# One chain per tile on compact 64x64 blocks, a modulation ring of its own, and the last expert added from PSUM

## The reference, cut to what matters

```python
cs = jax.nn.silu(c)
for l in range(DEPTH):
    mod = (cs @ w_ada[l] + b_ada[l])[:, None, :]
    sh1, sc1, gt1, sh2, sc2, gt2 = jnp.split(mod, 6, axis=-1)
    h = rmsnorm(x, norm_mix[l]) * (1 + sc1) + sh1
    x = x + gt1 * mixer(h, ...)
    h = rmsnorm(x, norm_ffn[l]) * (1 + sc2) + sh2
    x = x + gt2 * (swiglu(h, ...) if l % 2 == 0 else moe(h, ...))
y = rmsnorm(x, norm_final) * (1 + scf) + shf
...
# gated delta-net, chunks of 64 tokens
m = jnp.where(strict, beta_h[..., :, None] * kk * lmask, 0.0)
t_inv = lax.linalg.triangular_solve(eye + m, eye, left_side=True, lower=True, unit_diagonal=True)
u = jnp.einsum('bnhts,bnshv->bnthv', t_inv, v * beta[..., None])
...
# experts
for e in range(N_EXPERTS):
    y = y + combine[..., e:e + 1] * swiglu(h, w_gate[e], w_up[e], w_down[e])
```

## Time and profile before

| | us |
|---|---|
| median of 3 executions | 2027.31 (2026.44 to 2028.02) |
| profiled execution, its own time | 2026.02 |
| its span in the trace | 2024.2 |
| TensorE busy (share of the span) | 1890.4 (93%) |
| VectorE busy | 1449.0 (72%) |
| ScalarE busy | 1100.7 (54%) |
| GpSimd busy | 12.6 (1%) |

### The profile page before, as it was taken

The page is one execution under the profiler, slowest core; times in us unless marked ns, Lnnn a source line. Parts: engine busy times, 40 slices in busy tenths (PEclk is TensorE's granted clock), DMA queues, the critical chain, the costliest instruction groups (busy, mean ns, idle before and its releaser), DMA issues.

```text
span 2024.2 us, 25108 instructions
## 1 busy us (share of the span) xinstructions
PE 1890.4 (93%) x10235; PEld 1552.2 (77%) x10235; DVE 1449.0 (72%) x1760; ACT 1100.7 (54%) x1101; POOL 12.6 (1%) x27
## 2 busy tenths in 40 slices
PE   5997899899999978987999999999999999999995
PEld 2995667899989956665778787787877878878783
DVE  2857647645448667476888788787887888888884
ACT  3754223333337642324667676775766767666772
POOL 0000000000000000000000000000000000000000
PEclk7997899999999988997999999999999999999997
DMA  9445374343352443732989899898998989989980
GB/s 374 155 138 180 123 265 156 136 147 115 128 197 105 149 177 107 276 135 103 365 331 349 326 355 335 330 355 319 354 341 326 361 325 339 351 318 362 334 316 27
DMA packets 92119, 505.29 MB, mean 250 GB/s; under 512 B 8064, under 2 KB 8224, under 8 KB 40544
## 3 DMA queue, kind: packets, MB, share of 16 engines
q1 hardware_dynamic: 89616, 488.29, 65.4%
q0 software_dynamic: 2384, 15.34, 2.0%
HBM read 494.88 MB, written 8.72 MB: 249 GB/s over the span
## 4 chain that ended last, share of the span: by engine, by line
issue 55%; PE 31%; DVE 10%; ACT 2%; SPq 1%; DMA 1%; POOL 0%; DVEq 0%; ACTq 0%; POOLq 0%
PE bank L610 30%; DVE wlo L424 1%; DVE work L1715 1%; DMA raw<-in_w_in 1%; SPq L524 1%; DVE wscr L1867 1%; PE bank L834 1%; ACT work L1248 0%; DVE work L1716 0%; DVE wscr L1939 0%; ACT L1248 0%; ACT whi L419 0%; SPq L533 0%; DVE work L1847 0%; DVE hl L1646 0%
## 5 line engine op out<-in xcount | busy, mean ns | idle before, releaser
L424 DVE TENSOR_TENSOR wlo<-raw,whi 128x2048 fp32r<-128x2048 f32 (+1 forms) x412 | 919.9, 2262 | 198.9 <-ACT whi L419 197.3
L419 ACT ACTIVATE whi<-raw 128x2048 fp32r<-128x2048 f32 (+1 forms) x412 | 761.7, 1889 | 79.8 <-PE bank L610 75.4
L610 PE MATMUL bank<-whi,hg_high 128*128 128x512 f32 x896 | 368.7, 411 | 1.5 <-DVE hg_low L2129 1.5
L610 PE MATMUL bank<-whi,hg_low 128*128 128x512 f32 x896 | 354.8, 396 | 0.0
L610 PE MATMUL bank<-wlo,hg_high 128*128 128x512 f32 x896 | 354.5, 396 | 0.0
L610 PE MATMUL bank<-hh,whi 128*128 128x320 f32 x944 | 298.5, 316 | 23.4 <-DVE hl L1637 17.2
L610 PE MATMUL bank<-hh,wlo 128*128 128x320 f32 x944 | 293.6, 311 | 0.0
L610 PE MATMUL bank<-hl,whi 128*128 128x320 f32 x944 | 293.5, 311 | 0.0
L1248 ACT ACTIVATE work<-bank 128x512 f32<-128x512 f32 (+3 forms) x217 | 101.0, 487 | 262.3 <-PE bank L610 231.8
L610 PEld LDWEIGHTS bank<-hh,whi 128*128 128x128 f32 x944 | 179.6, 190 | 30.9 <-issue 22.3
L610 PEld LDWEIGHTS bank<-whi,hg_high 128*128 128x128 f32 x896 | 168.8, 188 | 43.1 <-issue 4.4
(11 more groups left out here) (262 smaller groups left out, 1860.6 us busy)
## 6 DMA issues: line engine op xcount, KB each, us to landing
raw<-in_moe SPq DMA_DIRECT2D x336, 1024.0 KB, 4.8
raw<-in_ada SPq DMA_DIRECT2D x56, 1024.0 KB, 5.4
raw<-in_w_in SPq DMA_DIRECT2D x30, 1024.0 KB, 4.8
raw<-in_gu SPq DMA_DIRECT2D x22, 1024.0 KB, 4.8
raw<-in_down SPq DMA_DIRECT2D x16, 704.0 KB, 4.0
raw<-in_w_out SPq DMA_DIRECT2D x8, 1024.0 KB, 5.2
work<-in_s_gdn POOLq DMA_DIRECT2D x2, 2048.0 KB, 12.2
out_gdn_s<-work POOLq DMA_DIRECT2D x2, 2048.0 KB, 7.4
```

The costliest lines, as they stand in the source:

```text
L419: ac.activation(whi[:, part(n), 0:width(n)], raw[:, n % SLOTS, 0:width(n)], ACT.Copy).then_inc(S("w_high"), 1)
L424: ve.tensor_tensor(wlo[:, n % SLOTS, 0:width(n)], raw[:, n % SLOTS, 0:width(n)], whi[:, part(n), 0:width(n)], ALU.subtract).then_inc(S("w_ ...
L610: return pe.matmul(out, lhsT, rhs, start=start, stop=stop, **k)
```

## The change

**Inversion.** Tiles 0 and 1 now have one chain each. Up to v = 5 it works on the two diagonal 64x64 blocks of each head alone: the block of rows 0 to 63 and that of rows 64 to 127 stand in the same 256 columns, four heads side by side. TensorE handles the blocks one by one, alternating between the quarter of the array with rows and columns 0 to 63 and that with rows and columns 64 to 127; the transposes of the second quarter are products with the identity. One mask and one update on DVE, and one copy on ACT, cover all four heads. Level 6 (`LAST`) only computes the 64x64 block that lies off the diagonal: four transposes, four products, ACT's copy, four products, and a negation on DVE. Some set-up is added (a unit block, a copy of the level table, a cleared quarter), and the strict matrix is written in blocks.

**Modulation.** Each modulation group and weight has its place in a list, `RING`, from which SP issues. Group 1 stays ahead of the inversion of layer 0 and group 2 in its levels. Group 3 has six loads behind the sums of squares of layer 0's output, two in the dense FFN (u = 2 and 3), and its turn at u = 5. Group 4 has six behind the sums of squares of the dense FFN, two in layer 1's projection (u = 3 and 4), its turn at u = 8. Group 5 stands ahead of layer 1's inversion. Group 6 has six behind the sums of squares of layer 1's output and two at the start of the experts.

**End.** The residual of experts 0 to 6 runs on DVE in the last expert, the last expert goes from PSUM into x, the flag is loaded before that, the squares and their sums come ahead of the branch, and y is stored in four parts.

```diff
+def ring_order():
+
+    def ada(x, *ks):
+        yield from (("ada", x, k) for k in ks)
+
+    def weights(first, n):
+        yield from (("w", first + i) for i in range(n))
+
+    yield from ada(0, *range(KD))
+    yield from weights(AT_IN[0], H_IN)
+    yield from ada(1, *range(KD))
+    yield from ada(2, *range(KD))
+    yield from weights(AT_OUT[0], H_OUT)
+    for x, first, n in ((3, AT_GU, H_GU + H_DN), (4, AT_IN[1], H_IN)):
+        yield from ada(x, 0)
+        yield from weights(first, 1)
+        yield from ada(x, 1, 2, 3, 4, 5)
+        yield from weights(first + 1, 3)
+        yield from ada(x, 6, 7)
+        yield from weights(first + 4, n - 4)
+    yield from ada(5, *range(KD))
+    yield from weights(AT_OUT[1], H_OUT)
+    yield from ada(6, *range(KD))
+    yield from weights(AT_MOE, len(MOE))
...
-        IBANK = (NB[0:2], NB[2:4], XB[1:2])
+        IBANK = (NB[0], NB[1], XB[1])
+        INV = [(t[4][:, 256:], t[4][:, 0:256], t[5][:, 0:256], t[5][:, 256:], t[7]) for t in DSET[0:2]]
+        INV.append((DSET[2][3], DSET[2][4], DT2[:, 0:256], DU2[:, 0:256], DY2))
...
-        ABANK = B[1]
+        ABANK = [B[1], B[1], B[1], B[7], B[3], B[1], B[7]]
...
-            yield from ((i, hs, v) for i in range(2) for hs in range(2))
+            yield from ((i, v) for i in range(2))
             if 2 <= v < 2 + LEVELS[2]:
-                yield 2, 0, v - 2
-
-        def chain(i, hs):
-
-            nt = TILES[i][1]
-            heads = (2 * hs, 2 * hs + 1) if i < 2 else range(NH)
-            return nt, heads, slice(heads[0] * nt, (heads[-1] + 1) * nt), IBANK[i][hs]
+                yield 2, v - 2
...
+            for at, what in enumerate(RING):
+                if at >= SLOTS:
+                    gone = RING[at - SLOTS]
+                    if gone[0] == "w":
+                        sp.wait_ge(*used(gone[1]))
+                    else:
+                        sp.wait_ge(S("ada_mm"), KD * gone[1] + gone[2] + 1)
...
-            po.wait_ge(S("y_done"), 1)
-            store(O["y"], hT[:], "y_out")
+            po.wait_ge(S("hs_norm"), 5)
+            for k in range(1, KD, 2):
+                po.wait_ge(S("h_norm"), KD + k + 1)
+                store(O["y"][:, k - 1:k + 1, :], hT[:, k - 1:k + 1, :], "y_out")
...
+                    def turned(o, m, r):
+
+                        return mm(o, m, ident[r, r]) if r.start else pe.transpose(o, m, ident[r, r])
...
+                            bank, (_, MB, TC, UC, YC) = IBANK[i], INV[i]
+                            if (i, x) in AT_MASK:
...
+                            if x == LAST:
+                                DM, DU = DSET[i][3], DSET[i][6]
+                                for h in range(NH):
+                                    pe.transpose(bank[0:64, 64 * h:64 * h + 64], DU[0:64, P * h:P * h + 64], ident[0:64, 0:64])
+                                for h in range(NH):
+                                    ins = mm(bank[0:64, 256 + 64 * h:320 + 64 * h], DM[64:P, P * h:P * h + 64],
+                                             DU[64:P, P * h + 64:P * h + P])
+                                ins.then_inc(S("dy_mm"), 1)
+                                continue
+                            for h in range(NH) if x > 1 else ():
+                                for r in blocks(i):
+                                    turned(bank[r, 64 * h:64 * h + 64], UC[r, 64 * h:64 * h + 64], r)
+                            for h in range(NH):
+                                for r in blocks(i):
+                                    o, m = bank[r, 256 + 64 * h:320 + 64 * h], MB[r, 64 * h:64 * h + 64]
+                                    if x:
+                                        ins = mm(o, m, UC[r, 64 * h:64 * h + 64])
+                                    else:
+                                        ins = turned(o, m, r)
                             ins.then_inc(S("dy_mm"), 1)
-                        for i, hs, x in chains(v):
+                        for i, x in chains(v):
                             if x == 0:
                                 continue
-                            nt, heads, _, bank = chain(i, hs)
-                            DT, DY = DSET[i][5], DSET[i][7]
-                            after(pe, "dy", l, AT_UPDATE[i, hs, x])
-                            for h in heads:
-                                c = slice(h * nt, (h + 1) * nt)
-                                o = (h - heads[0]) * nt
-                                ins = mm(bank[0:nt, o:o + nt], DT[0:nt, c], DY[0:nt, c])
+                            bank, (_, MB, TC, UC, YC) = IBANK[i], INV[i]
+                            after(pe, "dy", l, AT_UPDATE[i, x])
+                            for h in range(NH):
+                                for r in blocks(i) if x < LAST else (slice(0, 64),):
+                                    c = slice(64 * h, 64 * h + 64)
+                                    ins = mm(bank[r, c], TC[r, c], YC[r, c])
...
-                        ada(x + 1, *((0,), (1, 2), (3, 4), (5, 6), (7,))[v - 2])
+                    if v > 1 and l == 0:
+                        ada(2, *((0,), (1, 2), (3, 4), (5, 6), (7,))[v - 2])
...
-                ada_turn(x + 1)
+                if l == 0:
+                    ada_turn(2)
                 heads_spread(("heads", 2 * l + 1))
                 after(pe, "gdn_state", l, 1)
                 new_values(1)
-                ada(x + 2, 0)
                 keys(2)
-                ada(x + 2, 1)
                 after(pe, "do", l, 1)
                 outputs(1)
-                ada(x + 2, 2, 3)
                 new_values(2)
-                ada(x + 2, 4)
                 after(pe, "do", l, 2)
                 outputs(2)
-                ada(x + 2, 5)
                 after(pe, "do", l, 3)
                 heads_sum(("heads", 2 * l + 2), w(4 * TL, TL))
-                ada(x + 2, 6, 7)
                 heads_spread(("heads", 2 * l + 2))
-                ada_turn(x + 2)
...
+                ada((3, 6)[l], 0, 1, 2, 3, 4, 5)
                 if l == 0:
 
                     for u in range(FD):
@@ -1018,6 +1055,10 @@
                                 ins = mm3(B[2 * b + u % 2][:, 0:T], wh[:, k, c], wl[:, k, c], hh[:, k, :], hl[:, k, :],
                                           k == 0, k == KD - 1)
                         ins.then_inc(S("gu_mm"), 1)
+                        if u in (2, 3):
+                            ada(3, u + 4)
+                        if u == 5:
...
+                    ada(4, 0, 1, 2, 3, 4, 5)
...
+            for j in range(KD):
+                sum_squares(5, hT, j)
...
-                def masked(i, hs, v):
-
-                    (nt, heads, c, _), (DM, DMB) = chain(i, hs), DSET[i][3:5]
-                    nh = len(heads)
+                def masked(i, v):
+
+                    nt, (MC, MB, _, _, _) = TILES[i][1], INV[i]
                     if v:
-                        after(ve, "dy_mm", l, AT_LEVEL[i, hs, v - 1])
-                    lev = v3(cbf("level", nt), 7)
-                    do(tt(v3(DMB[0:nt, c], nh), v3(DM[0:nt, c], nh), mid(lev[:, v, 0:nt], nh), ALU.mult), "dmb")
+                        after(ve, "dy_mm", l, AT_LEVEL[i, v - 1])
+                    lev = v3(cbf("level", nt), 7)[:, v, 0:64]
+                    do(tt(v3(MB[0:nt, 0:256], 4), v3(MC[0:nt, 0:256], 4), mid(lev, 4), ALU.mult), "dmb")
...
+                            if x == LAST:
+                                do(ts(full[0:64, :, 64:], v3(bank[0:64, 0:256], 4), -1.0, None, ALU.mult), "dtu")
+                            elif i < 2 and x == LAST - 1:
+                                for r in blocks(i):
+                                    ins = tt(full[r, :, r], v3(UC[r, :], 4), v3(bank[r, 0:256], 4), ALU.subtract)
+                                    go(ins) if r.start == 0 else do(ins, "dtu")
+                            else:
+                                do(tt(UC[0:nt, :], UC[0:nt, :], bank[0:nt, 0:256], ALU.subtract), "dtu")
...
+                if e == NE - 1 and c in (3, 4) and (kind, b) in SPREAD:
+                    j = 4 * (c - 3) + SPREAD.index((kind, b))
+                    ve.wait_ge(S("e_scatter"), KD * (NE - 1))
+                    residual(hT[:, j, :], j, 48 + 40, None)
...
+            more = ve.value_load(flag[0:1, 0:1], min_val=0, max_val=1)
             for j in range(KD):
-                ve.wait_ge(S("e_sc_mm"), KD * (NE - 1) + j + 1)
-                scattered(j, B[4 + j % 2]).then_inc(S("e_scatter"), 1)
-            ve.wait_ge(S("e_scatter"), KD * NE)
-
-            more = ve.value_load(flag[0:1, 0:1], min_val=0, max_val=1)
+                n, bank, gate = KD * (NE - 1) + j + 1, B[4 + j % 2], md(48 + 40)
+                xs = v3(xT[:, j, TP:], NSEQ)
+                ve.wait_ge(S("e_sc_mm"), n)
+                go(stt(xT[:, j, 0:TP], bank[:, 0:TP], gate[:, j, 0:1], xT[:, j, 0:TP], ALU.mult, ALU.add))
```

(3 more changed lines are left out.)

293 lines of the change are left out of this document (154 added, 139 removed).

## The result

The changed kernel takes 2042.26 us (median of four, 2037.9 to 2048.93); the kernel before, in the same runs, 2027.06. The ratio is 1.0078 with a 95% interval of 1.0062 to 1.0094. Forecast was 1983, and a range of 1971 to 2004. The profiled execution took 2037.9, its span is 2036.0, 11.8 us longer than before. Another series on one chip gave 2038.29 beside 2026.03, 1.0078 again (1.0048 to 1.0109).

What follows compares the result with a forecast made beforehand. TensorE fills the expert stage; in the inversions no engine is full and a chain alternating between engines sets the end. Inversion -32.7, output stages -8.0, added loads +5.0 and tail -8.5 sum to -44.2: 1983 us, range 1971 to 2004.

Steps and rivals of the forecast that it cites:

- The turns of a tile: Inversion, a tile's first phase: transposes and identity products in alternating quarters overlap, the longer half setting 0.92 us.
- the forecast gain of 12.6: Layer 0's inversion: level by level, shorter TensorE chains and fewer DVE mask-and-update pairs sum to -12.6 us.
- 128*64 products: Evidence for overlap: products alternating between the array's column halves take 0.7 us for eight 128-column passes, not 0.9.
- Rival D: Inversion: each switch between quarters empties the array, some 480 switches at 0.25 us, +120, 2103; chance 0.04.
- Rival B: Inversion: the quarters don't overlap, both blocks going to one PSUM bank; gain 13.7 for 32.7, time 2002; chance 0.22.
- Rival C: Mixer: less work between waits drops TensorE's clock to 1.2 GHz in more of it, 1993 to 2002; chance 0.11.
- Layer 1's loads: Layer 1's inversion: eight modulation loads of group x+1 leave its levels, -7.5 us.
- Output stages: Both layers' output stages: modulation group x+2 leaves, with its turn and DVE adds, -3.8 and -4.2, together -8.0 us.
- The norm gaps: Norms: six loads each of groups 3, 4 and 6 hide in TensorE's 6.07 us wait (5.18 at the router), 0.
- The FFN's +2.5: Dense FFN, a stage TensorE fills: two added loads and a turn cost 1.92 + 0.60, +2.5 us.
- The projection's +2.5: Layer 1's projection, a stage TensorE fills: two added loads and a turn cost 1.92 + 0.60, +2.5 us.
- The end, -8.5: Tail: residuals under the experts start the root's refinement 6.2 us earlier, the four-part store saves 2.3; -8.5 in all.

Runs made afterwards that it cites:

- identity products and group 6: Changed kernel with identity products for all transposing passes in levels 0 to 5 and group 6's loads in layer 1's inversion levels: 1996.8 us.

## Why the prediction was wrong, by its steps

**The turns of a tile, "0.92 ... 4 x 4 passes": the step that failed.** The sum took a transposing pass and an identity product as two passes that overlap when they use different quarters. They don't: a pair takes 0.43, measured, for 0.115, and a tile's first phase 2.18 for 0.92. At level 0 and at levels 2 to 5 that is 12.6 us a layer at full clock, which alone eats up the forecast gain of 12.6. Layer 0's profiles agree: 64.5 with the transposing passes and 51.9 without. In layer 1 it is 75.3 and 49.2, 13.6 more than that price, at a clock of 0.53 in the one and 0.75 in the other.

The rest of the inversion's sum held where the clock did. In the kernel with identity products and group 6, at a clock of 0.93 beside 0.94 before, layer 0's inversion is 12.5 shorter than in the kernel before, level by level (from the start of a level's first pass to that of the next level's, level 6 up to `keys`):

| levels of layer 0 | 0 and 1 | 2 | 3 | 4 | 5 | 6 | sum |
|---|---|---|---|---|---|---|---|
| forecast | -2.3 | -1.7 | -2.7 | -1.7 | -2.3 | -1.9 | -12.6 |
| identity products, group 6 | -2.4 | -1.7 | -2.9 | -2.1 | -2.1 | -1.3 | -12.5 |

Layer 1's inversion, which keeps eight loads in that kernel, is 12.4 shorter (48.6 for 61.1). With identity products alone the clock was 0.83 and 0.75, and the inversions gained 8.9 and 11.9 (51.9 and 49.2 against 60.8 and 61.1); that kernel, 1993.41, lies in the forecast's range. So the 3.7 that the changed kernel's layer 0 lost beyond the price were also lost without a transposing pass, at about the same clock. The evidence that the sum leaned on, 128*64 products, was of products with products, and that holds: 0.029 a pass.

**Rival D** had the sign and the kind of the mechanism (the array empties) and put it at the wrong place: it counted every change of quarter, 480, and priced it at 0.25. The steps that count are eight in a tile's phase, between transposing passes and products, at about 0.1 each and with the overlap lost, and the change of quarter between products is free. The argument against D was right about quarters and blind to the transposing passes; with it D got 0.04. **Rival B** is refuted by the identity products. **Rival C** came true beside it: the granted clock fell to 0.53 in layer 1. The prediction linked it to less work between waits. TensorE was busy for 60 of 67 us there, but at passes that the low clock itself makes longer, so that this link is neither shown nor refuted.

**Layer 1's loads, "-7.5".** Worth 1.9 with the old inversion, and nothing with identity products (49.2 without loads, 48.6 and 48.7 with eight). The sum priced the loads by their own length, those of level 3 at the low clock; they were the work on which the slow stretch behind a wait fell, and when they go, the next work takes that stretch.

**Output stages, -8.0:** -7.1 in the changed kernel, -8.8 with the old inversion, in which the moved modulation alone differs there. The mechanism held: the loads' part was worth more and the wait behind it longer. TensorE's row ahead of the spreading answers to the 3.14 of the earlier trace rows:

```profile
314.33 4.63 PE L636 MATMUL bank<-rs,cf 128*128 128x320 f32 x10 [5.98 <-DVE rt L1714]
```

**The norm gaps and added loads.** Right: the six loads fill the gap, and the wait falls from 6.07 to 0.78:

```profile
358.05 5.36 PE L636 MATMUL bank<-raw,small 128*32 128x512 f32 x48
364.19 0.38 PE L636 MATMUL bank<-hh,whi 128*128 128x320 f32 x1 [0.78 <-DVE hl L1694]
```

The FFN's +2.5 is +2.3. The projection's +2.5 is +4.4; a wait of TensorE for a split of DVE there is 2.9 where it was 1.3, and that 1.6 makes up most of the rest. The +2.4 ahead of layer 0, where no load was added, shows in some profiles (projection 112.3) and not in others of the same code (110.8), and its cause stays open.

**The end, -8.5:** -9.5, and -8.8 alone. DVE's and then ACT's timeline after the last expert:

```profile
2011.29 0.48 DVE L2270 SCALAR_TENSOR_TENSOR xT<-bank,mod,xT 128x256 f32<-128x256 f32 x1 [8.00 <-PE bank L636]
...
2023.00 0.49 DVE L1662 TENSOR_TENSOR rt<-rs 128x320 f32<-128x320 f32 x1 [0.85 <-ACT rs L1296]
...
2019.05 1.28 ACT L1296 ACT_TABLE_LOAD   x1
2020.34 0.20 ACT L1296 ACTIVATE warm<-warm 128x1 f32<-128x1 f32 x1
2021.04 1.28 ACT L1296 ACT_TABLE_LOAD   x1 [0.49 <-ACT warm L1296]
```

and the store's issues (count, KB each, us to landing):

```profile
out_y<-hT POOLq DMA_DIRECT2D x4, 320.0 KB, 3.0
```

From the last expert's first residual to the root's refinement it is 2023.00 - 2011.29 = 11.7 where 13.6 was forecast, though ACT loads its table a second time behind the branch, which the prediction hadn't seen. A part of y lands in 3.0 for the 2.5 taken.

**What stays open:** why the clock falls so far in one layer and not in the other of the same profile. The loads alone don't set it: layer 0 has had 0.64 and 0.84 with the same ones. With the transposing passes the inversions stood at 0.53 to 0.86, with identity products at 0.75 to 0.93, so that the passes may have a part in it; no run takes that apart.

## What to carry to other kernels

Before two kinds of TensorE instructions are assumed to overlap, find a row in which just these two kinds stand next to each other in that shape, and read the distance of their starts; a row of one kind beside itself says nothing about the pair. In quarters of the array, turn a block by a product with the identity and not by a transposing pass when products stand around it: it takes two passes for one, and here it was 45 to 49 us faster. Work that lay in a slow stretch of the clock wasn't saved by its own length when it was moved: the stretch fell on what came next (1.9 us for 7.5).

## What the runs showed of the hardware

- Products of two quarters that share neither rows nor columns of the array overlapped fully into one PSUM bank: sixteen passes of 64 columns in 0.47 us, 0.029 each, where one quarter alone takes 0.058.
- In quarters a step between a transposing pass and a product cost about 0.1 us more than the pass (0.77 for seven); over the whole array it cost nothing (0.11 a pass on either side of the step).
- TensorE was busy for 60.15 of 67.30 us in layer 1's inversion and was granted 0.53 of its clock, most of it at 1.2 GHz; the same profile has 0.83 in layer 0's, and a second profile of the kernel 0.69 in both (`keys` included).
